# Swapped key columns in a shared tile, slabs split at other times, and a shorter hand-over from attention to merge

## The chip, the cores and the metric

The kernel runs on one core of one Trainium2 chip. The metric is the device time of one execution in microseconds (us). Kernels are compared by the median of several executions. A core has five engines that run side by side and meet at semaphores: TensorE (PE, matmuls), VectorE (DVE), ScalarE (ACT), GpSimd (POOL) and SyncE (SP, which here issues all transfers from HBM). All data is fp32. A matrix product is made of three matmuls: each operand is split into a high part, rounded for the matrix unit, and a low part, the rest; high x high, high x low and low x high are added in PSUM.

## The reference

Two networks run one after another on 512 tokens of width 1024, each with two layers. Cut to what matters here:

```python
def first_block(x, ...):                       # two layers
    u = rmsnorm(h, attn_norm[l])
    h = h + hybrid_mixer(u, ...)               # three attentions, gates, w_o
    u = rmsnorm(h, mlp_norm[l])
    h = h + square(relu(u @ w_up[l])) @ w_down[l]

# hybrid_mixer, its end
g = sigmoid(gates)
merged = (g[:, :, 0] * (o_a @ w_a) + g[:, :, 1] * (o_b @ w_b) + g[:, :, 2] * (o_c @ w_c))
return merged @ w_o

def hybrid_layer(x, w_in, ...):                # second network, two layers
    h = x @ w_in
    sb_cols, mla_cols, rwkv_cols = split(h)
    mix = concat([stick_breaking(sb_cols), mla_mixer(mla_cols), rwkv7_mixer(rwkv_cols)]) @ w_o
    x = layer_norm(ALPHA * x + mix)
    u_act, u_gate = split(x @ ffn_w_up)
    return layer_norm(ALPHA * x + (gelu(conv(u_act)) * u_gate) @ ffn_w_down)

# mla_mixer, its start: 192 + 128 + 32 columns
c_q, c_kv, k_rope = split(cols, [MLA_Q_LORA, MLA_Q_LORA + MLA_KV_LORA])
k_rope = apply_rope(k_rope, cos, sin)          # [t1*cos - t2*sin, t2*cos + t1*sin]
```

## The kernel before

The activations lie with the 1024 features on partitions, as eight chunks of 128 x 512 tokens. The program is a row of blocks, one after another; at the end of a block all engines meet. A first-network layer has a projection block, an attention block (the tiles of q, k and v come from the projection), a merge block (gates, the three branch products, w_o) and an MLP block. A second-network layer has a projection block, an attention block (stick-breaking and MLA), a recurrence block (RWKV) and a block with w_o, layer norm and the feed-forward part. Semaphores are of two sets that blocks use in turn; a block's end clears the set that was just used.

**Slabs.** Weights come from HBM in slabs of 128 x 2048 (1 MB), in a ring of two to four buffers named raw_a, raw_c, raw_f, raw_p or raw_d by the stage. For each slab ScalarE writes the high part (w_hi), and VectorE or GpSimd the low part (w_lo, raw minus w_hi); then PE uses it. The first two slabs of a block (AHEAD = 2) are fetched and split in the block before. For the second network's projection this is done by fetch_next2 (SyncE: parameters, then two slabs), next_hi2 (ScalarE, line 464) and next_lo2 (VectorE, line 469).

**Projection of the second network** (lines 1508 to 1745). Eleven slabs in the order SLABS2 hold two tiles of 128 output columns each; tile n of the list TILES is 24 matmuls (lines 396 to 398). Slab 1 holds the two tiles of MLA's query columns: cq tile 0 is 128 columns, tile 1 is 64 query columns, then the 32 key columns for rope on partitions 64 to 95, then 32 of zeros. Slab 2 holds the tile ckv and the tile krs, which is zeros but for the 32 key columns with halves swapped. Rope of the key is kr * cos + krs * sin, on VectorE (lines 1729 to 1731). ScalarE evicts each tile from PSUM (lines 1637 and 1641); GpSimd makes the low part of every slab from the third on (line 1685). LORA_AT, KK_AT, KKROOT_AT and CHAIN_AT say after which tile the side work of the recurrence is done.

**Attention of the first network** (lines 825 to 1085). 36 units of two heads and 128 queries go through a pipeline; a step of its loop has unit s0 at the logits, s1 at the exponentials, s2 at the scaling and turn of the weights, s3 at the values, s4 at the output. GpSimd multiplies the weights by the inverse denominators (line 1019, semaphore scaled), PE turns them (line 939, for dilated units 936), ScalarE or VectorE copies them to pt, PE multiplies by the values (line 960), ScalarE and VectorE keep high and low parts of the output (lines 1001 and 1072). The last two units are of the top-k attention, 512 keys wide. SyncE fetches the two first slabs of the merge block once the last dilated unit's logits are done.

**Start of the merge block.** PE first counts all banks up by one, so that waits can be written as if each bank had been used once. ScalarE writes the high part of the first 1024 columns of slab 0 (FIRST), then of the rest; VectorE the low parts (line 1219); PE waits for the first low part (part_lo).

**End of a second-network layer.** Eleven down slabs; slab m is split when PE has used slab m - 2 (split_down_hi, split_down_lo, with a row mean taken off by down_mean). Then, in layer 0, ScalarE splits the two next slabs behind the last down slab's split; VectorE adds the down product into h chunk by chunk (line 2950) and makes their low parts behind the first and the third addition. ScalarE squares h (line 2823), GpSimd adds up six of the squares (line 2836), PE sums over features (line 278), and the inverse root goes out through line 299 on. The end of the first network's last MLP block is built alike, with the low parts ahead of all additions.

## Time and profile before

| | us |
|---|---|
| median of three runs | 3522.18 |
| lowest, highest | 3518.57, 3523.44 |
| profiled execution, its time | 3520.51 |
| profiled execution, its span | 3518.7 |
| PE busy in it | 3375.3 (96%) |
| DVE, ACT, POOL busy | 1708.7, 1353.9, 982.5 |
| granted PE clock, mean | 0.976 |

All times in a view are microseconds from the start of the span. A matmul of 512 columns is listed with 0.39 us, but they overlap: at full clock one starts every 0.227 us, at half clock every 0.427. A row of the timeline has start, length, engine, line, instruction, out<-in, shapes, count, and in brackets how long the engine stood idle before it and what ended that. A "q" behind the engine means its sequencer, as for SyncE's transfers.

### The profile page before, as it was taken

The numbers are of one execution on the slowest core, as the hardware profiler recorded it, in microseconds if no ns is written. First come the engines' busy times: TensorE is split into PE (matmuls) and PEld (weight loads), VectorE is DVE, ScalarE is ACT, GpSimd is POOL, SyncE is SP. The second block draws the span as 40 slices with busy tenths as digits, with TensorE's granted clock in tenths as the row PEclk, the third lists the DMA queues.
The fourth block names the chain that finished last, engine by engine and source line by source line (L and its number), as shares of the span: only waits on it lengthen the run. The fifth ranks groups of instructions, "written<-read, shape, count | busy, mean of one in ns | idle before, by whom it ended". The sixth has DMA issues, their size and how long they took to land. (4 is left out here: it accounts for less than half of the span.)

```text
span 3518.7 us, 55538 instructions
## 1 busy us (share of the span) xinstructions
PE 3375.3 (96%) x22968; PEld 2773.4 (79%) x22968; DVE 1708.7 (49%) x2662; ACT 1353.9 (38%) x2059; POOL 982.5 (28%) x641
## 2 busy tenths in 40 slices
PE   8989999999999899999999999899998999899998
PEld 6777787888777778878887759888887768898887
DVE  4887334404249753441312656454454466454454
ACT  4646323313255453332224353343324443243322
POOL 2325002434433330034444341141102332232100
PEclk9999999999999999999999999899999999999999
DMA  3200222222222012223232200212222200012222
GB/s 141 91 30 27 89 102 86 96 96 96 96 96 72 1 54 100 102 85 107 92 110 105 72 1 4 76 58 95 96 96 91 84 13 3 29 73 105 95 96 72
DMA packets 38820, 267.04 MB, mean 76 GB/s; under 512 B 4800, under 2 KB 5184, under 8 KB 7616
## 3 DMA queue, kind: packets, MB, share of 16 engines
q1 hardware_dynamic: 38592, 263.74, 21.1%
q8 instruction: 174, 2.85, 0.3%
q14 instruction: 54, 0.44, 0.0%
HBM read 261.63 MB, written 2.10 MB: 75 GB/s over the span
## 5 line engine op out<-in xcount | busy, mean ns | idle before, releaser
L1418 POOL TENSOR_TENSOR w_lo_f<-raw_f,w_hi_f 128x2048 fp32r<-128x2048 f32 x60 | 275.9, 4598 | 384.6 <-ACT w_hi_f L384 384.6
L396 PE MATMUL ps<-u_hi,w_hi_d 128*128 128x512 f32 (+1 forms) x768 | 290.6, 378 | 7.8 <-POOL u_lo L2842 6.2
L398 PE MATMUL ps<-u_hi,w_lo_d 128*128 128x512 f32 (+1 forms) x768 | 286.8, 373 | 0.0
L397 PE MATMUL ps<-u_lo,w_hi_d 128*128 128x512 f32 (+1 forms) x768 | 286.7, 373 | 0.0
L384 ACT ACTIVATE w_hi_f<-raw_f 128x2048 fp32r<-128x2048 f32 x64 | 121.9, 1908 | 255.1 <-PE ps L398 243.8
L396 PE MATMUL ps<-u_hi,w_hi_f 128*128 128x512 f32 x512 | 201.7, 394 | 6.6 <-POOL u_lo L334 6.6
L607 POOL TENSOR_TENSOR w_lo_a<-raw_a,w_hi_a 128x2048 fp32r<-128x2048 f32 x30 | 137.9, 4600 | 229.3 <-ACT w_hi_a L603 229.3
L397 PE MATMUL ps<-u_lo,w_hi_f 128*128 128x512 f32 x512 | 201.1, 393 | 0.0
L398 PE MATMUL ps<-u_hi,w_lo_f 128*128 128x512 f32 x512 | 201.1, 393 | 0.0
L396 PE MATMUL ps<-hid_hi,w_hi_f 128*128 128x512 f32 x512 | 199.2, 389 | 0.0
L397 PE MATMUL ps<-hid_lo,w_hi_f 128*128 128x512 f32 x512 | 199.2, 389 | 0.0
L398 PE MATMUL ps<-hid_hi,w_lo_f 128*128 128x512 f32 x512 | 199.2, 389 | 0.0
L1445 DVE TENSOR_TENSOR hid<-hid 128x512 f32<-128x512 f32 x64 | 116.1, 1814 | 145.1 <-ACT hid L1394 144.0
L396 PE MATMUL ps<-u_hi,w_hi_a 128*128 128x512 f32 x432 | 172.7, 400 | 6.3 <-POOL u_lo L334 6.3
L396 PEld LDWEIGHTS ps<-u_hi,w_hi_d 128*128 128x128 f32 x768 | 146.1, 190 | 36.1 <-POOL u_lo L2842 8.1
L398 PE MATMUL ps<-u_hi,w_lo_a 128*128 128x512 f32 x432 | 169.5, 392 | 0.0
L397 PE MATMUL ps<-u_lo,w_hi_a 128*128 128x512 f32 x432 | 169.2, 392 | 0.0
L397 PEld LDWEIGHTS ps<-u_lo,w_hi_d 128*128 128x128 f32 x768 | 146.5, 191 | 25.6 <-issue 0.5
L398 PEld LDWEIGHTS ps<-u_hi,w_lo_d 128*128 128x128 f32 x768 | 146.3, 190 | 25.0
L2854 POOL TENSOR_TENSOR hid_lo<-ge,hid_hi 128x512 f32 (+1 forms) x44 | 57.2, 1300 | 385.2 <-ACT hid_hi L2799 385.2
L396 PE MATMUL ps<-u_hi,w_split_c 128*128 128x512 f32 x384 | 151.0, 393 | 7.3 <-DVE w_split_c L1219 7.3
L687 ACT ACTIVATE ps<-ps 32x512 f32<-32x512 f32 x208 | 117.3, 564 | 103.6 <-PE ps L398 53.6
(441 smaller groups left out, 8600.1 us busy)
## 6 DMA issues: line engine op xcount, KB each, us to landing
raw_d<-in_w SPq DMA_DIRECT2D x70, 1024.0 KB, 4.8
raw_f<-in_w SPq DMA_DIRECT2D x64, 1024.0 KB, 4.8
raw_c<-in_w SPq DMA_DIRECT2D x40, 1088.0 KB, 5.0
raw_a<-in_w SPq DMA_DIRECT2D x36, 1024.0 KB, 4.9
raw_p<-in_w SPq DMA_DIRECT2D x24, 1024.0 KB, 4.8
wo_raw<-in_w SPq DMA_DIRECT2D x4, 1024.0 KB, 6.1
cst<-in_cst SPq DMA_DIRECT2D x1, 2112.0 KB, 10.2
h<-in_x SPq DMA_DIRECT2D x8, 256.0 KB, 4.6
```

What stands on the lines that cost most here:

```text
L384: nc.scalar.activation(hi[:, k % 2, 0:width], raw[:, k % raw.shape[1], 0:width], ACT.Copy).then_inc(S["w_hi"], 1)
L396: nc.tensor.matmul(out, w_hi, x_hi, start=start, stop=False)
L397: nc.tensor.matmul(out, w_hi, x_lo, start=False, stop=False)
L398: return nc.tensor.matmul(out, w_lo, x_hi, start=False, stop=stop)
L607: eng.tensor_tensor(WA_lo[:, i % 4, :], WA_raw[:, i % 4, :], WA_hi[:, i % 3, :].bitcast(F32), ALU.subtract)\
L687: nc.scalar.activation(halves[32 * q:32 * q + 32, i % 2, :], src[32 * o:32 * o + 32, :], ACT.Copy).then_inc(S["swapped"], 1)
L1418: nc.gpsimd.tensor_tensor(WF[2][:, k % 2, :], WF[0][:, k % 2, :], WF[1][:, k % 2, :].bitcast(F32), ALU.subtract).then_inc(S["w_lo"], 1)
L1445: nc.vector.tensor_tensor(x, x, x, ALU.mult).then_inc(S["relu_kept"], 1)
L2854: nc.gpsimd.tensor_tensor(at(hid2_lo, k), ge, at(hid2_hi, k).bitcast(F32), ALU.subtract)\
```

## The change

There are five edits.

1. The 32 swapped key columns go into the zeros of cq tile 1 (partitions 96 to 127), and the tile krs is dropped from TILES. The host lays the weights out as before; slab 1 is now fetched in two transfers, all but the last 32 of each 256 columns, and those 32 from slab T2_KRS // 2. The sine table is fetched to partitions 96 to 127 as well. Slab 2 holds one tile; slab 3's low part is made by VectorE. The places of the recurrence's side work move up by one tile, but for LORA_AT, SUM_AT and ROOT_AT.
2. In the first attention VectorE scales the last two units (BY_DVE), not GpSimd.
3. ScalarE and VectorE split the first 1024 columns of merge slab 0 within the last steps of the attention block. PE no longer waits for part_lo.
4. SyncE, not PE, counts the banks at the start of the merge block, ahead of come_ahead.
5. At the end of second-network layer 0, the parameters for NORM_GAIN are copied ahead of the down slabs' loop; the first next slab is split behind down slab 9 (NEXT_AT), the second one on ScalarE behind the last down matmul's slab_used and on VectorE behind the last addition.

```diff
@@ fetch_next2, next_hi2
             for i in range(AHEAD):
-                sy.dma_start(WP_raw[:, i, :], d["w2"][layer:layer + 1, SLABS2[i], :, 0:2048].rearrange("a p c -> p (a c)"))\
-                  .then_inc(S["ahead"], 16)
+                to = WP_raw[:, i, :].rearrange("p (k c) -> p k c", c=256)
...
+                if SLABS2[i] == T2_CQ // 2:
+                    sy.dma_start(to[:, :, 0:SWAP_TO], cols(T2_CQ // 2, 0, SWAP_TO)).then_inc(S["ahead"], 16)
+                    sy.dma_start(to[:, :, SWAP_TO:256], cols(T2_KRS // 2, SWAP_AT, RD)).then_inc(S["ahead"], 16)
+                else:
+                    sy.dma_start(to, cols(SLABS2[i], 0, 256)).then_inc(S["ahead"], 16)
-            act.wait_ge(S["ahead"], 16 * (AHEAD + 1))
+            act.wait_ge(S["ahead"], 16 * (AHEAD + 2))
@@ first attention, PE / ACT / POOL / DVE
+                            if k in BY_DVE:
+                                pe.wait_ge(S["scaled_dve"], 2 * BY_DVE.index(k) + 1 + cs[-1] // n)
...
+                        if s2 == len(units) - 4:
+                            act.wait_ge(S["ahead"], 32)
+                            nc.scalar.activation(WC[1][:, 0, 0:FIRST], WC[0][:, 0, 0:FIRST], ACT.Copy).then_inc(S["first_hi"], 1)
...
+                        if k in BY_DVE:
+                            continue
...
+                            if k in BY_DVE:
+                                x, w = exps(k)
+                                dve.wait_ge(S["den_ready"], k + 1)
+                                for e in range(2):
+                                    nc.vector.tensor_scalar(x[:, e, 0:w], x[:, e, 0:w], per_unit(INV_AT, k)[:, e:e + 1], None, ALU.mult)\
+                                      .then_inc(S["scaled_dve"], 1)
+                            if k == len(units) - 1:
+                                dve.wait_ge(S["first_hi"], 1)
+                                nc.vector.tensor_tensor(WC[2][:, 0, 0:FIRST], WC[0][:, 0, 0:FIRST], WC[1][:, 0, 0:FIRST].bitcast(F32),
+                                                        ALU.subtract)
@@ merge block
+                    banks_counted(sy)
                     come_ahead(sy)
...
-                    for b in range(8):
-                        pe.sem_inc(full[b], 1)
-                        pe.sem_inc(read[b], 1)
...
-                                if (it, q, j) == (0, 0, 0):
-                                    pe.wait_ge(S["part_lo"], 1)
@@ projection of the second network
-            TILES = [2 * k + half for k in SLABS for half in range(2)]
+            TILES = [2 * k + half for k in SLABS for half in range(2) if 2 * k + half != T2_KRS]
...
-            LORA_AT, KK_AT = [4 + p for p in range(PAIRS)], [9 + p for p in range(PAIRS)]
+            LORA_AT, KK_AT = [4 + p for p in range(PAIRS)], [8 + p for p in range(PAIRS)]
...
-            CHAIN_AT = [13, 15, 17, 19]
+            CHAIN_AT = [12, 14, 16, 18]
...
+                        if n == AT[T2_CKV]:
+                            i = HALF + 1
+                            dve.wait_ge(S["w_hi"], i + 1)
+                            nc.vector.tensor_tensor(WP_lo[:, i % 3, :], WP_raw[:, i % 3, :], WP_hi[:, i % 2, :].bitcast(F32),
+                                                    ALU.subtract).then_inc(S["slab_lo_dve"], 1)
@@ end of a second-network layer
                         split_down_hi(act, m)
+                        if m == NEXT_AT and layer < DEPTH - 1:
+                            next_hi2(act, 0)
...
-                        for i in range(AHEAD):
-                            next_hi2(act, i)
+                        next_hi2(act, 1)
...
                         split_down_lo(dve, m)
-                    nc.vector.tensor_copy(small[:, NORM_GAIN:NORM_GAIN + 2 * DC], prm[:, P2_LN2G:P2_LN2G + 2 * DC])\
-                      .then_inc(S["kept_prm"], 1)
+                        if m == NEXT_AT and layer < DEPTH - 1:
+                            next_lo2(dve, 0)
...
-                        if n in (0, 2) and layer < DEPTH - 1:
-                            next_lo2(dve, n // 2)
+                    if layer < DEPTH - 1:
+                        next_lo2(dve, 1)
```

VectorE at the end of the first attention and the start of the merge block, before. sc_68 and sc_69 are the weights of units 34 and 35, L1048 the logits' eviction, L1072 low parts of outputs, w_split_c the parts of merge slab 0 and 1.

```order
L1048 ISA small 128x1
L1072 TENSOR_TENSOR o_lo<-ps,o_hi 128x128
L1084 RECIPROCAL small<-small 128x2
L1072 TENSOR_TENSOR o_lo<-ps,o_hi 128x128
L1084 RECIPROCAL small<-small 128x2
L1072 TENSOR_TENSOR o_lo<-ps,o_hi 128x128 x4
L887 UNCONDITIONAL_BRANCH
L1213 UNCONDITIONAL_BRANCH
L1219 TENSOR_TENSOR w_split_c<-raw_c,w_split_c 128x1024
L1219 TENSOR_TENSOR w_split_c<-raw_c,w_split_c 128x1152
```

The same place in the changed kernel.

```order
L1072 ISA small 128x1
L1096 TENSOR_TENSOR o_lo<-ps,o_hi 128x128
L1108 RECIPROCAL small<-small 128x2
L1113 TENSOR_SCALAR sc_68<-sc_68,small 128x512 x2
L1096 TENSOR_TENSOR o_lo<-ps,o_hi 128x128
L1108 RECIPROCAL small<-small 128x2
L1113 TENSOR_SCALAR sc_69<-sc_69,small 128x512 x2
L1117 TENSOR_TENSOR w_split_c<-raw_c,w_split_c 128x1024
L1096 TENSOR_TENSOR o_lo<-ps,o_hi 128x128 x4
L903 UNCONDITIONAL_BRANCH
L1240 UNCONDITIONAL_BRANCH
L1245 TENSOR_TENSOR w_split_c<-raw_c,w_split_c 128x1152
```

Four scalings came in, and the first half of the split went from behind the block's end to ahead of the last four low parts.

VectorE at the end of second-network layer 0, before: L2565 is the low part of a down slab, L469 of a next slab, L2950 an addition into h.

```order
L2565 SCALAR_TENSOR_TENSOR w_lo_d<-raw_d,small,w_hi_d 128x1024 x2
L2946 COPY small<-prm 128x16
L2950 SCALAR_TENSOR_TENSOR h<-h,ps 128x512
L469 TENSOR_TENSOR w_lo_p<-raw_p,w_hi_p 128x2048
L2950 SCALAR_TENSOR_TENSOR h<-h,ps 128x512 x2
L469 TENSOR_TENSOR w_lo_p<-raw_p,w_hi_p 128x2048
L2950 SCALAR_TENSOR_TENSOR h<-h,ps 128x512 x5
```

The same place in the changed kernel, with the mean of down slab 10 left in.

```order
L2604 SCALAR_TENSOR_TENSOR w_lo_d<-raw_d,small,w_hi_d 128x1024 x2
L482 TENSOR_TENSOR w_lo_p<-raw_p,w_hi_p 128x2048
L2591 TENSOR_REDUCE small<-raw_d 128x2
L2594 TENSOR_SCALAR small<-small 128x2
L2604 SCALAR_TENSOR_TENSOR w_lo_d<-raw_d,small,w_hi_d 128x1024 x2
L2992 SCALAR_TENSOR_TENSOR h<-h,ps 128x512 x8
L482 TENSOR_TENSOR w_lo_p<-raw_p,w_hi_p 128x2048
```

The first next slab's low part now stands ahead of the work on down slab 10, the second one behind all eight additions.

SyncE at the same layer's end, before and then changed.

```order
L2637 DMA raw_d<-in_w 128x2048
L455 DMA prm<-in_prm 128x165
L458 DMA raw_p<-in_w 128x2048 x2
L2633 UNCONDITIONAL_BRANCH
L1541 UNCONDITIONAL_BRANCH
```

```order
L2676 DMA raw_d<-in_w 128x2048
L462 DMA prm<-in_prm 128x165
L472 DMA raw_p<-in_w 128x2048
L469 DMA raw_p<-in_w 128x8x224
L470 DMA raw_p<-in_w 128x8x32
L2672 UNCONDITIONAL_BRANCH
```

The second slab became two transfers with eight pieces per partition each.

## Rows read from the trace of the kernel before

**Rows 1.** The page, busy time, share and instructions of each engine.
```profile
PE 3375.3 (96%) x22968; PEld 2773.4 (79%) x22968; DVE 1708.7 (49%) x2662; ACT 1353.9 (38%) x2059; POOL 982.5 (28%) x641
```
**Rows 2.** PE's waits: total us, times, longest.
```profile
PE ps L278 <- POOL qsum L2836: 6.5, 2, 5.9
```
**Rows 3.** Timeline, ACT, projection of second-network layer 0.
```profile
1914.09 0.60 ACT L1637 ACTIVATE cq<-ps 128x512 f32<-128x512 f32 x1 [2.38 <-PE ps L398]
...
1919.52 0.60 ACT L1637 ACTIVATE ckv<-ps 128x512 f32<-128x512 f32 x1 [2.52 <-PE ps L398]
```
**Rows 4.** Timeline, low parts on POOL and DVE, and DVE's idle stretch.
```profile
1865.56 4.49 DVE L469 TENSOR_TENSOR w_lo_p<-raw_p,w_hi_p 128x2048 fp32r<-128x2048 f32 x2 [71.90 <-ACT w_hi_p L464]
...
1916.57 4.58 POOL L1685 TENSOR_TENSOR w_lo_p<-raw_p,w_hi_p 128x2048 fp32r<-128x2048 f32 x1 [6.18 <-ACT w_hi_p L1622]
...
1933.80 0.75 DVE L1707 SCALAR_TENSOR_TENSOR rw_in<-ps,prm,rw_in 128x511 f32<-128x511 f32 x1 [28.99 <-ACT rw_in L1641]
```
**Rows 5.** Timeline, attention's end and merge's start, layer 0; last a group by form.
```profile
338.78 1.03 SPq L222 DMA_DIRECT2D raw_c<-in_w  x2
...
351.44 0.60 ACT L1005 ACTIVATE pt<-ps 128x512 f32<-128x512 f32 x1 [1.36 <-PE ps L939]
...
353.14 6.19 POOL L1019 TENSOR_SCALAR sc<-sc,small 128x512 f32<-128x512 f32 x4 [1.35 <-DVE small L1084]
353.38 0.66 PE L960 MATMUL ps<-pt,cv 128*64 128x128 f32 x8
...
359.97 1.97 PE L960 MATMUL ps<-pt,av 128*64 128x128 f32 x32
...
362.36 0.29 DVE L1072 TENSOR_TENSOR o_lo<-ps,o_hi 128x128 fp32r<-128x128 f32 x1 [0.58 <-ACT o_hi L1001]
...
365.57 0.76 PE L396 MATMUL ps<-u_hi,w_split_c 128*128 128x512 f32 x1 [3.63 <-DVE w_split_c L1219]
...
L1740 DVE TENSOR_SCALAR asig<-asig,prm 128x512 f32<-128x512 f32 x8 | 3.9, 487 | 0.3
```
**Rows 6.** Stretches: us, busy PE, PEld, DVE, ACT, POOL, then clock, DMA, GB/s.
```profile
362.00:365.50 3.50, 0.00 (x0) 0.00 (x0) 1.75 (x3) 2.81 (x4) 0.00 (x0) 0.95 0.00 0
365.50:368.60 3.10, 3.03 (x7) 2.48 (x8) 2.63 (x2) 2.75 (x2) 0.00 (x0) 0.50 0.30 51
```
**Rows 7.** Timeline and a transfer's time, end of second-network layer 0.
```profile
2649.79 0.34 SPq L2637 DMA_DIRECT2D raw_d<-in_w  x1
...
2669.04 2.48 DVE L2565 SCALAR_TENSOR_TENSOR w_lo_d<-raw_d,small,w_hi_d 128x1024 fp32r<-128x1024 f32 x2 [6.00 <-ACT w_hi_d L2546]
...
2688.08 0.39 PE L398 MATMUL ps<-hid_hi,w_lo_d 128*128 128x512 f32 x1
...
2699.68 0.16 DVE L299 TENSOR_SCALAR small<-ps 128x4 f32<-128x4 f32 x1 [7.28 <-PE ps L278]
...
raw_d<-in_w SPq DMA_DIRECT2D x70, 1024.0 KB, 4.8
```
**Rows 8.** Timeline, end of second-network layer 1, PE and DVE.
```profile
3502.75 0.39 PE L398 MATMUL ps<-hid_hi,w_lo_d 128*128 128x512 f32 x1
...
3507.38 0.16 DVE L299 TENSOR_SCALAR small<-ps 128x4 f32<-128x4 f32 x1 [3.51 <-PE ps L278]
```
**Rows 9.** Transfers in 917.9:918.5 (132 B), 1850.2:1852.2 (660 B), 1860:1862.5 (8 KB); an issue near 2671.6.
```profile
q1 hardware_dynamic: 144, 0.02, 27.2%
...
q1 hardware_dynamic: 161, 0.12, 18.0%
...
q1 hardware_dynamic: 145, 1.06, 100.8%
...
prm<-in_prm SPq DMA_DIRECT2D x1, 82.5 KB, 1.9
```
**Rows 10.** Timeline, end of the first network, ACT and PE.
```profile
1863.61 3.72 ACT L464 ACTIVATE w_hi_p<-raw_p 128x2048 fp32r<-128x2048 f32 x2 [5.32 <-DMA raw_p<-in_w]
...
1879.51 1.02 PE L278 MATMUL ps<-cst,hid 128*128 128x2 f32 x8 [1.57 <-POOL hid L289]
```

73 lines of the change are left out of this document (45 added, 28 removed).

## The prediction, made before the changed kernel was run

> **What bounds the kernel now.** I read the page first: TensorE (PE) is busy for 96% of the span [rows 1]. So time can be won in two ways only: fewer matmuls, or fewer microseconds in which PE stands still. The list of PE's waits (who waited, for whom, in total, times, longest) tells which stops are large and what releases them; the sum at the end of a layer of the second network stands there with 6.5 us in two stops, 5.9 of it in one [rows 2]. Two stops of one line that differ so much are a question by themselves. Then I read the timeline at the four places that the diff names, engine by engine, and lastly the granted clock. The profiled execution took 3520.5 us (span 3518.7, 1.8 around it). The sum below is made against 3520.5, which is 1.7 under the median of the three runs shown.
>
> **Part 1, one tile fewer in each second-network projection.** The tile of swapped key columns was 24 matmuls of 128x512. Evictions of neighbouring plain tiles start 5.43 us apart, 1914.09 to 1919.52 [rows 3]; that is 24 matmuls at full clock, one every 0.227 us. PE has no stop inside this stage, so each layer loses 5.4 us: 2 x 5.4 = **10.9 us**. ScalarE's eviction of the tile goes too, under PE and worth nothing. The risk is the supply of weights: slab 2 now holds one tile, so slab 3 is wanted 5.4 us sooner. Its low part was made by GpSimd from 1916.57 to 1921.15 [rows 4]. PE would want it when the key tile is done and the first two decay matmuls are through, after 1919.5: up to 1.6 us late. The change gives this subtraction to VectorE, which is idle for 29.0 us before 1933.80 and does two such slabs in 4.49 us, 2.3 each [rows 4]: 1916.6 to 1918.9, in time, with 0.6 us or more to spare. All later slabs keep their distance to PE. Rope of the key part moves one tile earlier on the same idle VectorE. No cost.
>
> **Part 2, the tail of the first attention.** The last two units are scaled by GpSimd in one run of 6.19 us, four instructions of 1.55 [rows 5]. PE turns each half as it comes, and its last values end at 361.94, 359.97 + 1.97. VectorE does a 128x512 multiplication by a column in 0.49 us [rows 5]. Its scaling of unit 34 can start at 353.1, where GpSimd's did, and end at 354.1; unit 35 follows two microseconds later and stays ahead of PE. Then PE is the pace: it is free at 354.04 (353.38 + 0.66), turns 0.65 + 0.65 for unit 34, values 0.66, turns 0.65 + 0.65 for unit 35, and does the last values in 1.97, which ends at 359.3. **2.6 us** less in each layer. New on VectorE behind it is the first half of the merge split, about 1.2 us; behind that stand only the low parts of outputs whose matmuls end later still. New on ScalarE is the high part, 1.06 us, ahead of a copy at 351.44 for which ScalarE had waited 1.36 us [rows 5]: it fits. Its data must have landed; the transfer is issued at 338.78 [rows 5], eleven microseconds before.
>
> **Part 3, the start of the merge block.** Now: PE's last matmul ends at 361.94, the last low part at 362.65 (362.36 + 0.29), then ScalarE copies, VectorE subtracts, and PE starts at 365.57 [rows 5]. With both done before the block, PE waits for the block's start alone and for the first count of a bank. ScalarE's first copy began 0.30 us after the last low part, behind SyncE's counts, so I put PE at +0.4. 365.57 - 362.65 - 0.4 = **2.5 us** per layer. The sixteen counts cost PE nothing before, since it waited for the split anyway; left on PE they would now show. On SyncE they stand ahead of come_ahead, for which ScalarE's first copy waits. No row gives a count's price; between nothing and 0.1 us each I allow the 0.1, 1.6 us in all. Then the second half's copy and subtraction (1.2 and 1.4 us) end near +4.5 us, and PE wants them after 24 matmuls, at +5.8. Hidden, by 1.3 us, and with it what stands behind on SyncE, the first refill of a slab. If the cover is gone, PE stops for the difference, once a layer. Parts 2 and 3: 2 x 5.1 = **10.2 us**.
>
> **Part 4, the clock behind it.** In 362 to 365.5 PE did nothing, and in 365.5 to 368.6 the granted clock was 0.50 (1.2 GHz), 7 matmuls in 3.1 us [rows 6]. At full clock these seven take 1.6. With the change PE stands still for only about 1.1 us there. I take it that the fall goes away: 2 x 1.4 = **2.8 us**. If not, this term is nothing. The Trainium skill ("TensorE: Matmul & The Clock Gate", Part 1) says that the throttled state is the default and that activity releases it; by that rule, the trace agrees, the fall follows the idle stretch, and the sum is the one with 2.8.
>
> **Part 5, from layer 0 to layer 1 of the second network.** In layer 0 the last matmul starts at 2688.08 and the token sum is read at 2699.68, 11.60 us later [rows 7]. In layer 1, where nothing is split ahead, it is 3502.75 to 3507.38, 4.63 us [rows 8]. The difference, **7.0 us**, is what the two slabs cost at this place: their two subtractions stand between VectorE's additions of h, and ScalarE's squares stand behind the copies. After the change the first slab is split under matmuls one slab earlier, ScalarE does the second before the first square is due, and VectorE's second subtraction stands behind the last addition: 2.3 us inside the 4.6 in which PE sums. So layer 0 should look like layer 1. The transfers are issued some 21 us sooner, right behind that of down slab 10. What is late next is down slab 10: ScalarE and VectorE touch it only after the early split. Its low part ends at 2671.52 now [rows 7]; PE wants it 48 matmuls, 10.9 us, before its last one ends, at 2677.4. Working back through a low part, a high part and a mean of up to 2.5 us each [rows 7] and the early split (1.9 [rows 10] and 2.3 [rows 4]), the transfers must have landed by 2665.7. Slab 10's transfer is issued at 2649.79 and takes 4.8 [rows 7], to 2654.6. Of the 11.1 us left, the parameter block wants about 0.3, a whole slab 2.5 and a second one 2.5: 6 us of room for pieces to be slower.
>
> **Part 6, a slab in 2048 pieces.** The second slab ahead is now 1024 pieces of 896 bytes and 1024 of 128 bytes instead of 128 rows of 8 KB. No transfer of such pieces is in the trace. The nearest packets [rows 9]: of 8 KB, 100.8% of 16 engines for 2.5 us and about 129 packets, 0.31 us each; of 660 bytes, 18.0% of 16 x 2.0 us for 128 and a few others, about 0.04; of 132 bytes, 27.2% of 16 x 0.6 us over 144, about 0.02. An engine gets 64 of either kind. Low end: 64 x (0.048 + 0.018) = 4.2 us against 8 x 0.31 = 2.5, so 1.7 more; in the best case nothing is lost or gained, since the bytes are the same. High end: the 128-piece parameter block took 1.9 us from issue to landing [rows 9]; if pieces came at that pace whatever the engines do, 2048 take 30 us, 28 more. I take 2.5, near the packets' own times, since those are measured at work and most of the 1.9 us of a small transfer is there for a large one too. Between the layers this hides (6 us of room). At the end of the first network it doesn't: ScalarE waited 5.32 us for this very transfer and started at 1863.61, VectorE's two subtractions and additions follow, and PE waits at 1879.51 for GpSimd's sum of what they give [rows 10]. So **2.5 us are lost** there, once. The Trainium skill ("DMA: Bandwidth & Descriptors", Specifications) speaks against this edit: it wants 512 bytes and more for line rate. The trace's 132-byte packets move far fewer bytes per time than the 8 KB ones, which agrees; taken to its end it makes the 128-byte pieces the slow ones, which is rival (a). The constants' transfer, now in three parts, is issued ahead of the slabs' and wanted behind the last down slab's split: hidden, unless its parts cost more than the slab's.
>
> **The sum.** 10.9 + 10.2 + 2.8 + 7.0 - 2.5 = 28.4; 3520.5 - 28.4 = **3492.1 us**.
>
> **Rivals.** (a) Pieces are moderately slow, 6 to 12 us more than the slab was. The end of the first network loses that, and above 6 us the room between the layers is gone too. At 6: 3.5 less gain, 3496; at 10: 7.5 and 4 of a stall at slab 10, 3504. For it: four times as many packets in flight per engine as anywhere in the trace; against it: their short times. (b) Slower than before: the pieces come one after another at the parameter block's pace. 28 lost at the end of the first network, and 28 - 6 = 22 of stall at down slab 10; 30.9 gained otherwise, so 3520.5 - 30.9 + 50 = 3540. It decides from about 18 us more per transfer. (c) The tail of the attention doesn't shorten, because VectorE's scaling waits for something I don't see or another bank comes late: parts 2 to 4 shrink by 5.2 and the clock's 2.8, 3500. (d) The clock falls at the merge as before, 3494.9; inside the forecast's range.
>
> **How the numbers follow.** My forecast, with (d) in it: 0.80. (a): 0.09. (c): 0.07. (b): 0.02. The edits give nothing that can be seen, since the clock's falls shift or an unseen wait takes their place: 0.02. The clock rises at a different moment after each of the eight or so stops, and half a microsecond to 1.5 either way at each is 3 us in all; with the runs' own 2 us, and (d), the forecast reaches from 3486 to 3497. To leave no more than 2 in 10 out, the range goes on to (c): **3486 to 3501**. A measurement tells 0.2%, 7 us, from no change: faster 0.95 (forecast, (a), (c)), same 0.03, slower 0.02.
>
> **What would show it.** 352 matmuls of line 396 on w_hi_p become 336 and the stage has no stop of PE. The run of GpSimd at 353 is gone and PE's stop before the first merge matmul is near 1.1 us with the clock at 1.0 behind it. The stop of 5.9 us at the layer's end is about 0.6. ScalarE's wait at the end of the first network shows the pieces' price directly; if it grows by more than 6 us, part 6 was wrong. A new stop of PE at the last down slab would mean the same between the layers.

## The result, and the profile after

| | before | changed |
|---|---|---|
| median of the runs, us | 3520.38 (4 runs) | 3484.69 (4 runs) |
| lowest, highest | 3515.36, 3523.44 | 3483.63, 3485.89 |
| ratio, 95% interval | | 0.990 (0.9888 to 0.9912) |
| profiled execution, its span | 3518.7 | 3482.6 |
| PE busy in it | 3375.3 | 3354.8 |
| granted PE clock, mean | 0.976 | 0.979 |

The changed kernel is 35.7 us faster. The forecast was 3492.1, from 3486 to 3501: the direction was right, the gain was put at 28.4, and the time lies 1.3 us under the range. The spans of the two profiled executions differ by 36.1.

Every place that the forecast named changed about as it said. First the waits of PE (total us, times, longest), which answer to [rows 2], and the matmuls of the projection by form:

```profile
PE ps L402 <- SPq L229: 2.1, 2, 1.0
...
PE ps L284 <- POOL hid L295: 3.1, 2, 2.5
...
PE ps L284 <- POOL qsum L2876: 1.1, 2, 0.5
```
```profile
L402 PE MATMUL ps<-u_hi,w_hi_p 128*128 128x512 f32 x336 | 137.0, 408 | 8.0 <-POOL u_lo L1534 8.0
```

The stops of 5.9 us and of 3.6 us are gone; the one ahead of the sum at the end of the first network grew by 0.9 (1.57 in [rows 10], 2.50 now), and the 336 matmuls are one tile per layer fewer. Timeline of the changed kernel, end of the attention and start of the merge in layer 0 (columns as in [rows 5], to which it answers):

```profile
355.75 0.88 DVE L1113 TENSOR_SCALAR sc<-sc,small 128x512 f32<-128x512 f32 x2
...
356.55 1.22 DVE L1117 TENSOR_TENSOR w_split_c<-raw_c,w_split_c 128x1024 fp32r<-128x1024 f32 x1
...
357.60 1.97 PE L979 MATMUL ps<-pt,av 128*64 128x128 f32 x32
...
359.99 0.29 DVE L1096 TENSOR_TENSOR o_lo<-ps,o_hi 128x128 fp32r<-128x128 f32 x1 [0.58 <-ACT o_hi L1020]
...
360.61 0.50 PE L402 MATMUL ps<-u_hi,w_split_c 128*128 128x512 f32 x1 [1.04 <-SPq L229]
```

PE's last values end at 359.57; the merge starts 0.33 us after the last low part (359.99 + 0.29), where 2.92 lay before. The clock behind it stays at its upper level, which answers to [rows 6]:

```profile
360.50:363.90 3.40, 3.29 (x14) 2.74 (x15) 1.17 (x1) 2.38 (x2) 0.00 (x0) 1.00 0.00 0
```

End of second-network layer 0, as [rows 7]: from the last down matmul to the reading of the sum 4.66 us, 11.60 before.

```profile
2664.34 0.39 PE L404 MATMUL ps<-hid_hi,w_lo_d 128*128 128x512 f32 x1
...
2665.26 1.02 PE L284 MATMUL ps<-cst,qsum 128*128 128x2 f32 x8 [0.53 <-POOL qsum L2876]
...
2669.00 0.16 DVE L305 TENSOR_SCALAR small<-ps 128x4 f32<-128x4 f32 x1 [1.11 <-PE ps L284]
```

End of the first network, as [rows 10]. SyncE's three issues, ScalarE's wait for them, and PE's stop, now 2.50 us:

```profile
1840.14 0.35 SPq L472 DMA_DIRECT2D raw_p<-in_w  x1
...
1840.53 0.44 SPq L469 DMA_DIRECT2D raw_p<-in_w  x1
...
1841.01 0.58 SPq L470 DMA_DIRECT2D raw_p<-in_w  x1
...
1848.49 3.72 ACT L477 ACTIVATE w_hi_p<-raw_p 128x2048 fp32r<-128x2048 f32 x2 [6.27 <-DMA raw_p<-in_w]
```
```profile
1864.37 1.43 PE L284 MATMUL ps<-cst,hid 128*128 128x2 f32 x8 [2.50 <-POOL hid L295]
```

To get the terms I compared the start of every PE matmul with that of the same matmul before, and read where the difference (the offset) changes. It changes by these amounts at the places of the edits:

| term, us | forecast | read from the two traces |
|---|---|---|
| two tiles fewer | 10.9 | 10.9 |
| tail of the attention, two layers | 5.2 | 6.3 |
| start of the merge, two layers | 5.0 | 5.3 |
| clock behind it | 2.8 | 2.8 |
| end of layer 0, second network | 7.0 | 7.0 |
| slab in pieces, end of the first network | -2.5 | -1.5 |
| sum | 28.4 | 30.8 |

Two of these rows hold clock as well. At the end of layer 0, before:

```profile
2694.39 1.84 PE L278 MATMUL ps<-cst,qsum 128*128 128x2 f32 x8 [5.92 <-POOL qsum L2836]
```

Behind this stop the 24 matmuls of the sum took 5.29 us until the sum was read, at half clock (it is low from 2693.1), and 3.74 after (2665.26 to 2669.00): 5.4 of the 7.0 are the shorter stop, 1.6 are clock. Of the -1.5 at the end of the first network 0.9 is the stop, and 0.6 is that the clock falls nearer to the start of the sum. At full clock the rows therefore add up to 27.0 (10.9 + 6.3 + 5.3 + 5.4 - 0.9).

**5.3 of the 36.1 us stand in none of these rows.** They come at stops that are alike in both kernels. In what follows, a fall is the moment at which the granted clock goes to its lower level (1.2 GHz, 0.50), and a low stretch is the time until it is back at 1.00. The plainest is the stop ahead of the first network's MLP block in layer 0. Stretches before (590.5 on) and after (584.8 on); the columns are as in [rows 6]:

```profile
590.50:593.80 3.30, 1.92 (x16) 1.86 (x16) 1.12 (x4) 0.84 (x2) 0.28 (x1) 1.00 0.00 0
593.90:597.20 3.30, 1.12 (x4) 0.72 (x4) 1.71 (x4) 0.85 (x2) 0.17 (x1) 0.50 0.14 20
597.30:600.60 3.30, 2.15 (x5) 1.80 (x6) 3.22 (x5) 1.97 (x4) 2.65 (x2) 0.50 0.88 355
600.70:604.10 3.40, 3.40 (x9) 2.63 (x8) 2.86 (x5) 1.86 (x4) 2.43 (x2) 0.50 0.55 234
```
```profile
584.80:588.20 3.40, 2.23 (x19) 2.02 (x18) 0.77 (x3) 0.79 (x2) 0.00 (x0) 1.00 0.00 0
588.30:591.60 3.30, 0.01 (x1) 0.00 (x0) 2.83 (x4) 1.89 (x3) 1.34 (x2) 0.50 0.42 97
591.70:595.00 3.30, 3.30 (x8) 2.62 (x9) 3.26 (x6) 1.49 (x3) 2.39 (x2) 0.50 1.00 420
595.10:598.40 3.30, 3.30 (x16) 2.67 (x15) 2.34 (x4) 1.57 (x3) 1.57 (x2) 1.00 0.21 89
```

PE waits 3.33 us for the same subtraction in both. Before, the clock is at its lower level from 593.9 to 604.1, 10.2 us; after, from 588.2 to 595.1, 6.8 us. The work resumes at 598.45 and 591.64, so 5.7 us of it ran at half clock before and 3.4 after. That alone is 1.1 us, with no edit near it. Over all stops the clock is low for 172.3 us before and 148.6 after (the last stretch counted to its end, 2 us behind the last instruction).

### The profile page after: what moved, and what is told of

It is laid out like the page before. It is cut to its first block and busy times, and to the rows that moved or that the text cites. A ratio compares the mean times of both kernels' runs of the same rounds, so it can differ in the third digit from the quotient of the medians.

```text
span 3482.6 us, 55438 instructions
## 1 busy us (share of the span) xinstructions
PE 3354.8 (96%) x22920; PEld 2758.1 (79%) x22920; DVE 1715.5 (49%) x2672; ACT 1351.9 (39%) x2057; POOL 958.1 (28%) x631
## 5 line engine op out<-in xcount | busy, mean ns | idle before, releaser
L700 ACT ACTIVATE ps<-ps 32x512 f32<-32x512 f32 x208 | 117.3, 564 | 103.7 <-PE ps L404 53.7
L396 DVE TENSOR_TENSOR w_lo_d<-raw_d,w_hi_d 128x2048 fp32r<-128x2048 f32 x44 | 106.3, 2416 | 104.0 <-ACT w_hi_d L390 103.4
```

What stands on the lines that cost most here:

```text
L396: nc.vector.tensor_tensor(lo[:, k % 2, 0:width], raw[:, k % raw.shape[1], 0:width], hi[:, k % 2, 0:width].bitcast(F32), ALU.subtract).then ...
L700: nc.scalar.activation(halves[32 * q:32 * q + 32, i % 2, :], src[32 * o:32 * o + 32, :], ACT.Copy).then_inc(S["swapped"], 1)
```

## The experiments

All are built from the changed kernel where nothing else is said. Its time over two sets of four runs is 3484.69 and 3485.14; differences below are against 3484.9. The kernel before was run beside each set, with medians of 3520.1, 3517.2 (the four kernels on the end of layer 0, the tail, the split and the counts), 3518.1 (the two shifts and the first two candidates) and 3522.2 us (the rest). So differences across sets are sure to 2 or 3 us only, and for the second set may be that much too small; where less matters, the reading goes by the traces.

### Each kernel once more

The question is whether the 5.3 us come and go between executions, or belong to the programs.

> The kernel before, once more, for a second trace of it. The trace shown of before has 22 half-clock stretches, 172 us in all; the changed kernel has 20, 149 us. Two of the seven 3.4 us pieces fewer lie at the merge, where the change removes the stop, one at the end of layer 0 and one at the program's end; three net lie behind stops that the change doesn't touch (593.9 to 604.1 in before, 588.2 to 595.1 after, for one). Theory L (these are luck: how far the clock falls behind one and the same stop differs between executions of one program): this trace has some unchanged stops with a stretch longer or shorter by 3.4 us than the first trace, and PE's starts drift against it by 1 to 1.7 us at each; the single times spread over 4 us or more. Theory D (the falls belong to the program): the same 22 stretches with the same lengths, 172 us, and times within 2 us of 3520.5.

> The changed kernel once more, in more rounds. Theory L: the half-clock stretches behind unchanged stops differ by 3.4 us here and there from the first trace of it, and the median lies between 3483 and 3490, with single times up to 5 us apart. The gain that the terms carry is then 30.8 (tile 10.9, tail 6.3, start of merge 5.3, clock there 2.8, layer's end 7.0, less 1.5 for pieces) and the rest, up to 5 us, comes and goes. Theory D: the same stretches, 149 us, and a median of 3484.7 within 1.5; the 5.3 us that my terms don't hold are then a steady part of the gain.

Before again: 3521.08 (10 runs, 3513.69 to 3523.03). Changed again: 3485.14 (4 runs, 3484.07 to 3488.76), ratio 0.9899 (0.9883 to 0.9916). Of the 22 low stretches of before 19 have the same length in the second trace, of the 20 of the changed kernel 18. The stop shown above has 10.2 us in both traces of before and 6.8 in both of after:

```profile
596.20:606.30 10.10, 6.78 (x18) 5.15 (x18) 7.96 (x12) 5.04 (x8) 5.49 (x4) 0.50 0.55 208
```
```profile
589.30:596.00 6.70, 3.40 (x8) 2.75 (x9) 6.23 (x9) 3.41 (x6) 3.86 (x3) 0.50 0.72 262
```

Two others of the changed kernel are longer by 3.4 us in its second trace (17.1 where it was 13.7 at 1865 us, 6.8 where it was 3.4 at 2070), and its span is 3487.0. Neither theory holds as it was put: most falls belong to the program, two or three per execution move. The gain of 35 us is steady all the same, by the medians.

### Moving one stop and nothing else

Five or ten matmuls without a use go into the merge block of layer 0, some 140 us ahead of the stop shown above. Nothing else differs, so the stop only comes later.

```diff
                                 b = bank_to_fill(pe, jobs, ("gate", q, j), it)
+                                if (layer, it, q, j) == (0, 2, 0, 0):
+                                    for _ in range(5):        # and 10
+                                        nc.tensor.matmul(ps[:, b, :], w_hi[:, 0, :], u_hi[:, 0, :], start=True, stop=True)
```

> The changed kernel with 5 extra matmuls of 512 columns, without a use, in merge layer 0 (about 1.13 us at full clock), long before the stop at its end. Nothing else differs, and every later stop has the same cause and length. In ten traces the half-clock stretch behind this stop is 6.83 us long where the work resumes 2.8 to 3.7 us after the clock's fall, and 10.24 where it resumes 4.3 to 6.6 after it. In the changed kernel it resumes 3.39 after it. Phase theory: now 4.5 after it, so 10.24, and PE is 1.13 + 1.15 = 2.3 us later behind this stretch; behind the next one (950 us, 3.46 now) 2.3 to 2.9 later; at the end anything from 0 to 5, not the plain 1.1. Rival (the falls are the program's, a shift is only a shift): all stretches as before and 1.1 us more at every place.

> The same with 10 extra matmuls, 2.27 us. Phase theory: the work resumes 5.7 after the fall, stretch 10.24, or the clock falls one step later and the work resumes 2.2 after it, stretch 6.83: by both PE is 2.8 us later behind it, only 0.5 more than with 5; and at later stops the stretches differ from those of the changed kernel at several places, in both directions. Rival: 2.3 us more at every place, twice the shift of 5.

With 5: 3489.04 (3487.27 to 3490.81), with 10: 3491.36 (3487.31 to 3493.53). So 1.13 us of matmuls cost 4.1, and 2.27 cost 6.4, by medians of different sets, each sure to 2 or 3 us; what the clock does is read from the traces. The stop is the same 3.33 us, and the clock low for 10.2 us (587.1 to 597.4, and with 10 matmuls 587.9 to 598.1):

```profile
587.20:593.90 6.70, 2.75 (x8) 2.11 (x9) 5.04 (x8) 2.44 (x4) 2.92 (x2) 0.50 0.46 155
594.00:597.30 3.30, 3.30 (x9) 2.56 (x9) 3.25 (x5) 1.90 (x3) 1.81 (x2) 0.50 0.73 308
597.50:600.70 3.20, 3.20 (x16) 2.65 (x15) 0.69 (x1) 0.58 (x1) 0.55 (x1) 1.00 0.02 5
```
```profile
592.26 0.77 PE L402 MATMUL ps<-u_hi,w_hi_f 128*128 128x512 f32 x1 [3.33 <-POOL u_lo L340]
```

This work resumes 5.1 us after the fall, where it was 3.4. Against the changed kernel, PE was 0.97 us early ahead of the five matmuls in this execution, 0.16 late behind them, 1.37 late behind this stop and 2.43 late behind the next one. So 1.13 became 2.34 at the first stop, where the phase theory said 2.3, and 3.40 at the second, where it said 2.3 to 2.9; from there on the falls differ in both directions. With ten it is 2.26, then 3.23 behind both stops. The rival, 1.1 us at every place, is out. In the fourteen traces without extra matmuls under the stops, the five block changes of this kind (near 590, 950, 1510, 1870 and 2670 us) all follow one order, by how long after the fall the block's first product starts:

| start after the fall, us | clock low for, us |
|---|---|
| 2.5 to 3.9 | 6.8 |
| 4.0 to 7.0 | 10.2 |
| 8.2 to 10.7 | 13.7 |
| 10.8 to 13.6 | 17.1 |
| 16.0 | 20.5 |

So what a stop costs in clock goes by its moment as well as by its length, and 1 us more or less ahead of it changes that. The Trainium skill ("TensorE: Matmul & The Clock Gate", Part 1) has the low state as the default that activity releases; the traces agree, and they add that the release comes later for the same stop when its moment shifts.

### The first edit alone

The tile krs, the whole-slab transfer, GpSimd's split of slab 3 and the old places of the side work are put back.

```diff
-            TILES = [2 * k + half for k in SLABS for half in range(2) if 2 * k + half != T2_KRS]
+            TILES = [2 * k + half for k in SLABS for half in range(2)]
```

> The changed kernel with the first edit undone alone: the tile of swapped key columns is back, slab 1 comes in one transfer, GpSimd splits slab 3, the side work is one tile later. Terms theory: 10.9 slower for the two tiles, 1.5 faster at the end of the first network for the whole slab: 3484.7 + 9.4 = 3494.1. If the edit brings more than its matmuls (a better place of the side work, fewer clock falls behind it), 3497 or more; if the early supply of slab 3 costs something hidden in the trace, under 3492.

3494.03 (3490.76 to 3496.53), 9.1 slower; 9.4 was expected. Within the 2 or 3 us of such a difference this edit holds no hidden work.

### What the pieces cost

Slab 1 in one transfer (this leaves out the swapped columns, so its result is not that of the reference; only its time is read), and, as the other end, slab 0 in eight transfers of 128-byte pieces.

```diff
-                if SLABS2[i] == T2_CQ // 2:
-                    sy.dma_start(to[:, :, 0:SWAP_TO], cols(T2_CQ // 2, 0, SWAP_TO)).then_inc(S["ahead"], 16)
-                    sy.dma_start(to[:, :, SWAP_TO:256], cols(T2_KRS // 2, SWAP_AT, RD)).then_inc(S["ahead"], 16)
-                else:
-                    sy.dma_start(to, cols(SLABS2[i], 0, 256)).then_inc(S["ahead"], 16)
+                sy.dma_start(to, cols(SLABS2[i], 0, 256)).then_inc(S["ahead"], 16)
```

> The changed kernel with slab 1 of the second network's projection fetched in one transfer of 8 KB rows; its swapped columns are then the zeros of the host's layout, so that rope of the key lacks its second half. Terms theory: the transfer lands about 1.0 us earlier and one issue of 0.5 us less stands ahead, PE's stop at the end of the first network goes from 2.5 back to about 1.6 us, and 3483.2 (1.5 less) is read; nothing changes between the layers, where the transfers land 11 us ahead of their need. Forecast's own price for the pieces: 2.5 less, 3482.2. If the pieces slow other transfers as well (the third slab behind them), more than 3 us less.

> The changed kernel with slab 0 ahead of the second network's projection fetched in eight transfers of 1024 pieces of 128 bytes each, instead of one of 128 rows of 8 KB; slab 1 as in the changed kernel. One look. By the row of 132-byte packets (0.02 us each, 64 more per engine and transfer) it lands 8 x 1.2 = 9.4 us after the engines begin, 7 later than a whole slab; the eight issues of 0.6 us take 4.7 of it. By the change's own slab (1024 + 1024 pieces landed 1.0 us later than a whole one, half of it the second issue) 8 x 0.5 = 4 to 5 us later. If small pieces come one after another at the pace of a parameter block (1.9 us for 128), more than 100.

Whole slab: 3483.57 (3482.96 to 3485.82), 1.3 less. SyncE issues both at 1839.57 and ScalarE starts 7.16 us later, against 8.35 (1840.14 to 1848.49) in the changed kernel: the pieces cost 1.2 us, 0.6 of it the added issue. PE's stop is 1.35.

```profile
1839.57 0.82 SPq L468 DMA_DIRECT2D raw_p<-in_w  x2
...
1846.73 3.72 ACT L473 ACTIVATE w_hi_p<-raw_p 128x2048 fp32r<-128x2048 f32 x2 [5.09 <-DMA raw_p<-in_w]
```

Only pieces: eight issues in 5.99 us, 0.75 each where an issue of a whole slab takes 0.35, and ScalarE starts 13.34 us after the first issue, 5.0 later than in the changed kernel. One execution took 3491.78, 6.9 more; there is only this one.

```profile
1840.92 5.99 SPq L473 DMA_DIRECT2D raw_p<-in_w  x8
1846.95 0.75 SPq L469 DMA_DIRECT2D raw_p<-in_w  x1
1847.74 0.90 SPq L470 DMA_DIRECT2D raw_p<-in_w  x1
1854.26 3.72 ACT L478 ACTIVATE w_hi_p<-raw_p 128x2048 fp32r<-128x2048 f32 x2 [11.27 <-DMA raw_p<-in_w]
```

So 1 MB in 8192 pieces of 128 bytes costs 5.0 us more than in 128 rows, and the issuing alone takes 5.6 more, 6.0 against 0.35. Whether an issue of many pieces takes long by itself or waits for those ahead of it isn't shown: the two issues of slab 1 behind them also take longer here, 0.75 and 0.90 where they took 0.44 and 0.58.

### The end of layer 0 alone

```diff
-                        if m == NEXT_AT and layer < DEPTH - 1:
-                            next_hi2(act, 0)
...
-                        next_hi2(act, 1)
+                        for i in range(AHEAD):
+                            next_hi2(act, i)
...
+                        if n in (0, 2) and layer < DEPTH - 1:
+                            next_lo2(dve, n // 2)
```

> The changed kernel with the order at the end of second-network layer 0 put back: both next slabs split by ScalarE behind the last down slab's use, their low parts between VectorE's additions. The parameters' copy stays early, and so do the transfers. Terms theory: from the last down matmul to the reading of the token sum 11.6 us in place of 4.66, so 7.0 slower, 3484.9 + 7.0 = 3491.9. If half-clock stretches behind it, or behind later stops that are the same in both, grow too, up to 3 more; if they shrink, as little as 4 more than 3484.9.

3489.76 (3487.92 to 3491.19), 4.9 slower by the medians, not 7.0. The way from the last down matmul to the sum is 2668.21 to 2678.02, 9.81 us, so the place itself costs 5.2 and not 7.0 (3.6 as a longer stop, 1.6 as half clock in the sum behind it):

```profile
2672.73 0.56 PE L284 MATMUL ps<-cst,qsum 128*128 128x2 f32 x2 [4.14 <-POOL qsum L2875]
```

The transfers still come early here, and ScalarE begins 10.5 us ahead of the last down matmul (2657.75), where it began 8.7 ahead in the kernel before (2679.37, behind a wait for the transfers); the forecast's 7.0 is right for the whole edit, and about 1.8 of it is the earlier fetch.

### Tail, first half of the split, and bank counts, each undone

```diff
-            BY_DVE = (len(units) - 2, len(units) - 1)
+            BY_DVE = ()
```

> The changed kernel with the last two units of the first attention scaled by GpSimd again. Terms theory, by the two traces of before and after: PE's last values end 3.1 and 3.3 us later in the two layers, 3491.3. Forecast's own size: 2.6 each, 3490.1. The first half of merge slab 0 is then split under the wait for GpSimd, so the start of the merge doesn't change. A rival, that clock falls behind unchanged stops carry part of what the trace shows as the tail's gain: under 3488, or above 3494.

3495.81 (3494.45 to 3495.88), 10.9 slower where 6.3 was expected. PE waits for GpSimd as before, in four stops (the last two are shown), but here the clock falls amid them and the last values run at half of it, 3.68 us in place of 1.97:

```profile
360.70 1.09 PE L958 MATMUL ps<-cst,sc 128*128 128x128 f32 x4 [0.30 <-POOL sc L1043]
362.24 1.12 PE L958 MATMUL ps<-cst,sc 128*128 128x128 f32 x4 [0.45 <-POOL sc L1043]
363.28 3.68 PE L979 MATMUL ps<-pt,av 128*64 128x128 f32 x32
```

In the kernel before the fall came 3 us after these values. The rival of the expectation (above 3494) holds: an edit's worth depends on where the clock's falls lie in the kernel that it is made in.

```diff
 # the first half split in the merge block (ScalarE, VectorE), and on PE:
+                                if (it, q, j) == (0, 0, 0):
+                                    pe.wait_ge(S["part_lo"], 1)
```

> The changed kernel with both halves of merge slab 0 split within the merge block, and PE waiting for the first low part; SyncE still counts the banks. Terms theory: PE starts 2.65 us later in each layer and the clock falls there again for 1.4 us of cost, so 8.1 slower, 3493.0. ScalarE's first copy now waits for SyncE's sixteen counts as well (0.06 us each by the changed trace), up to 1 us per layer more: 3495. If the clock at the merge doesn't fall, 3490.

```diff
-                    banks_counted(sy)
                     come_ahead(sy)
...
+                    for b in range(8):
+                        pe.sem_inc(full[b], 1)
+                        pe.sem_inc(read[b], 1)
```

> The changed kernel with the sixteen bank counts back on PE. Theory: they are now the last thing ahead of PE's first merge matmul; at 0.06 us each, as SyncE's are spaced in the changed trace, PE starts 0.7 us later in each layer, 3484.9 + 1.4 = 3486.3, and no clock fall. If a count costs PE more (0.1 us), 3487.5. If the longer stop makes the clock fall behind it, up to 3489. Rival: nothing that can be seen, since the counts run while PE's last matmuls drain.

First half in the merge block: 3492.85 (3490.39 to 3496.22), 8.0 slower, as expected. Counts on PE: **3497.51** (3496.26 to 3498.64), 12.6 slower where 1.4 was expected. Here PE's first merge matmul comes 2.82 us after the last low part, though the low part that it needs has been there since 358.3; the profile names no releaser, only issue:

```profile
360.53 0.29 DVE L1096 TENSOR_TENSOR o_lo<-ps,o_hi 128x128 fp32r<-128x128 f32 x1 [0.58 <-ACT o_hi L1020]
361.12 1.16 ACT L1196 ACTIVATE w_split_c<-raw_c 128x1152 fp32r<-128x1152 f32 x1 [0.69 <-SPq L235]
...
363.64 0.76 PE L402 MATMUL ps<-u_hi,w_split_c 128*128 128x512 f32 x1 [3.54 <-issue]
```

With the split alone put back, SyncE's counts delay ScalarE's copy by 0.94 (1.24 after the last low part, 0.30 before), and PE starts at 363.21:

```profile
359.31 0.29 DVE L1093 TENSOR_TENSOR o_lo<-ps,o_hi 128x128 fp32r<-128x128 f32 x1 [0.58 <-ACT o_hi L1020]
360.84 1.06 ACT L1189 ACTIVATE w_split_c<-raw_c 128x1024 fp32r<-128x1024 f32 x1 [1.63 <-SPq L235]
...
363.21 0.80 PE L402 MATMUL ps<-u_hi,w_split_c 128*128 128x512 f32 x1 [4.33 <-DVE w_split_c L1242]
```

The four kernels side by side, from the end of the last low part to PE's first merge matmul, layer 0:

| us | split in the merge block | split ahead |
|---|---|---|
| PE counts | 2.92 (before) | 2.82 |
| SyncE counts | 3.61 | 0.33 (changed) |

Two causes of the same length lay side by side: either edit alone gives 0.1 us there or costs 0.7, both give 2.6 per layer. The semaphore events of the traces show the counts themselves. With the counts on PE the sixteen go from 361.19 to 363.60, 2.4 us or 0.15 each, and PE's first matmul follows at 363.64; SyncE's go from 360.54 to 361.45 in the changed kernel, 0.06 each. In the kernel before, the first low part was ready at 365.28 and PE's sixteenth count was done at 365.37, so the counts, not the split, ended last, by 0.1 us; the view names the split because it leaves counts out. Of the 12.6 us the later starts are 5.0. The other 7.6 are in the main clock: it falls at the merge again (3.4 us, twice), the stretches at 592 and 951 us are 10.2 again, as in the kernel before, and half of PE's busy time in all low stretches is 58.5 us, against 49.6 and 52.9 in the two traces of the changed kernel.

### Is all of the 5.3 the clock's?

Both kernels get the same matmuls without a use under their stops (they are shown with the candidates below), to have fewer falls in both.

> The changed kernel with all the extra matmuls of the last one, and nothing else (its first network ends as in the changed kernel): 3 us or so above it. It is one half of a pair with the kernel before made alike: with fewer half-clock stretches in both, the difference of the two shows what the five edits are worth without the clock's share at unchanged stops. Sum of the terms as read in the traces: 30.7 (28.0 without the fall at the merge, 2.8).

> The kernel before with the same extra matmuls (and SyncE counting the banks of the MLP block). If the 5.3 us that my terms leave open are half-clock time behind unchanged stops, this pair differs by 27 to 32. If they are work of the edits that I have not seen, it still differs by 35 to 36.

Changed: 3469.42 (3467.42 to 3471.5). Before: 3507.33 (3502.28 to 3511.74). They differ by 37.9, outside both expectations (27 to 32, 35 to 36). The pair is not clean: in the kernel before, the clock is low for 142.3 us, in the changed one for 104.3, and before's fall now lies in the attention's tail, as in the experiment above. So I took the clock out by estimate instead: half of the time that PE is busy in the low stretches, summed over each whole trace.

| kernel | span | clock low | PE busy in it | half of that | span less that |
|---|---|---|---|---|---|
| before | 3518.7 | 172.3 | 117.3 | 58.6 | 3460.1 |
| before, again | 3521.2 | 176.0 | 123.3 | 61.7 | 3459.5 |
| changed | 3482.6 | 148.6 | 99.1 | 49.6 | 3433.0 |
| changed, again | 3487.0 | 155.4 | 105.7 | 52.9 | 3434.1 |
| before, filled | 3509.8 | 142.3 | 111.4 | 55.7 | 3454.1 |
| changed, filled | 3466.8 | 104.3 | 77.0 | 38.5 | 3428.3 |

Less the clock, the edits save 26.2 us in the plain kernels (3459.8 to 3433.6) and 25.8 in the filled ones. The terms read at full clock from the first pair of traces were 27.0, where this table has 27.1 (3460.1 to 3433.0). The forecast's terms without its clock term are 25.6; that this is so near is in part luck, since 1.6 of its 7.0 for layer 0 was clock, while its tail was too small and its pieces too dear. The clock gives 8.9 in the plain pair and 17.2 in the filled pair. This is an estimate (a latency that PE only waits out isn't halved); that both pairs agree within 0.4 us while their clock shares differ by 8 is what it rests on. Applied to the single experiments it is less exact: with the end of layer 0 undone it gives 3439.0, 5.4 above the changed kernel where the stop grew by 3.6, and with ten matmuls added 3437.4, 3.8 above where they take 2.3. So it is good to about 2 us; hidden work of 5 us is not left.

### Candidates

The first one treats the end of the first network as the change treats layer 0 of the second; the next ones put matmuls without a use where PE stands still anyway.

```diff
-                            for i in range(AHEAD):
+                            for i in range(AHEAD if layer < DEPTH - 1 else 1):
                                 (next_lo if layer < DEPTH - 1 else next_lo2)(dve, i)
...
+                    if layer == DEPTH - 1:
+                        next_lo2(dve, 1)
                     token_inverse(dve, jobs, "sum", Signal(dve_own))
```

> A candidate: at the end of the first network the second low part of the next slabs is taken behind VectorE's additions, as the change does at the end of second-network layer 0. VectorE's first addition comes 2.2 us earlier; the later ones are paced by PE. Theory: PE's stop of 2.5 us before the token sum becomes about 1.3, 1.2 us less; with the clock behind it the median is 3481 to 3486. Rival: GpSimd's chain of five additions of squares is the bound and nothing changes.

3481.06 (3479.2 to 3484.07), 3.8 less. PE's stop goes from 2.50 to 0.63 us.

```diff
+        def warm(b, w, n):
+            for _ in range(n):
+                nc.tensor.matmul(ps[:, b, :], w[:, 0:P], w[:, 0:512], start=True, stop=True)
...
+                        if hf == 0:
+                            warm(jobs.at["up", 0][0], WF[1][:, 0, :], 6)
```

> A candidate, the last one plus matmuls without a use at the head of the blocks whose first product waits for the normed input (projection and MLP blocks, 6 or 7 of 512 columns each), under the stop of 3.1 to 4.0 us that is there anyway; SyncE counts the MLP block's banks, so that PE is free for them. Theory: the clock comes back one step of 3.4 us earlier at four or five of the five such places that have a fall (588, 947, 1506, 1865, 2667 us), 1.7 us each: 7 to 8.5 less, 3475 to 3478. Rival A: matmuls at half clock under the stop don't bring it back, and the median stays within 1 of the last candidate's. Rival B: at half clock they last longer than the stop, PE starts later, and it is slower by 1 to 3.

3474.42 (3473.07 to 3475.38), 6.6 under the last one, with 38 extra matmuls. SyncE counts the banks of the MLP block here, so that PE is free for them; what that brings by itself was not tried. At 1863 us the clock is low for 6.8 us in place of 13.7, at 2663 for 3.4.

> The last candidate (extra matmuls at the heads of the blocks) with more of them: 13 under the stop of 4.3 us for the last pair of value slabs in each first-network projection, 12 under the 3.4 us ahead of the first turn of each attention, 3 under each stop of 1.2 us for the inverse roots but the first. Theory (a stop that is filled with matmuls lets the clock not fall or rise sooner): the falls at 219, 254, 1137 and 1172 us go, 1.5 to 3 each, 6 to 10 less than 3474.4 together, and up to 1.7 at each of the five block changes: 3460 to 3467. Rival: the fills delay the work behind them where the clock is down already, 3472 or more.

**3466.92** (3462.58 to 3467.3), ratio to before 0.9844 (0.9828 to 0.9861): 18 us under the changed kernel, and the fastest one here. The extra matmuls, and the product behind them:

```profile
586.98 2.93 PE L411 MATMUL ps<-w_hi_f 128*128 128x512 f32 x6 [0.76 <-POOLq L1453]
589.70 0.63 PE L404 MATMUL ps<-u_hi,w_hi_f 128*128 128x512 f32 x1
```

The clock doesn't fall any more near 219 and 254 us, but it does at 270.5, for 6.8 us, where it stayed up before; in layer 1 the falls of the attention (1138, 1172) go without such a one. Rows near 219 and 254 us:

```profile
219.00:223.00 4.00, 3.67 (x15) 3.68 (x16) 3.90 (x8) 1.08 (x2) 0.27 (x1) 1.00 0.00 0
250.00:254.00 4.00, 4.00 (x31) 3.65 (x31) 3.01 (x11) 1.72 (x9) 1.67 (x4) 1.00 0.00 0
```

It is low for 111 us in all, and the kernel has 106 matmuls more than the changed one. What of the 14.1 us each place brings wasn't tried one by one.

## Why the prediction missed, step by step

- **Part 1** held: 10.9, no stop of PE in the stage, slab 3 in time. Undone, it gave 9.1 of 9.4.
- **Part 2** was 1.1 too small. The forecast put the end of the last values at 359.3, and they ended at 359.57, which looks close; but the profiled execution of the changed kernel was 0.8 us behind that of before when it came to the attention (its first turn at 253.92, not 253.12). Set against the same matmuls, the tail is 3.1 and 3.2 us shorter, not 2.6. The forecast added up listed lengths (0.65 for four turns, 0.66 for eight values), but a listed length overlaps the next group: by their starts eight turns take 1.03 and eight values 0.58. From the start of the last eight values before unit 34's turns to the end of all it had 5.9 us, and the changed kernel takes 5.19 (354.38 to 359.57).
- **Part 3** had the right sum, 5.0 for 5.3, by a wrong price. "Between nothing and 0.1 us each I allow the 0.1": a count takes SyncE 0.06 and PE 0.15. "The sixteen counts cost PE nothing before, since it waited for the split anyway" does not hold: they ended 0.1 us after the split's first part, so PE would have been just as late without the split. The forecast came out right because both edits are made together.
- **Part 4** held where it looked, 2.8. The step that failed is the one behind it, in "how the numbers follow": clock shifts at unchanged stops were taken as noise, "3 us in all", either way. They are mostly fixed in a program; here they were worth 5.3 on one side (by the estimate above the clock is worth 8.9 in all: these 5.3, the merge's 2.8, 1.6 in layer 0's sum, less 0.6 at the end of the first network). With the 2.4 us by which the other terms were too small, that is more than the range allowed. The forecast also spoke of "eight or so stops", where the trace of before has 22 low stretches.
- **Part 5** held to 0.1 us. But what it called the cost of two slabs in VectorE's and ScalarE's way is 5.4 us of stop and 1.6 of half clock in the sum; and 5.2 of the 7.0 are the order, 1.8 the earlier fetch, which the forecast had put on the order alone.
- **Part 6** was 1.0 too dear. The packets' own times gave 1.7 more for the pieces; they took 1.2 with the added issue in it. The 2.5 was 0.8 put on top for what no row showed. The room between the layers was not needed: the low part of slab 10 ended at 2649.05, 4.6 us before PE wanted it.
- **The rivals**: (a) and (b) need pieces 6 or 18 us slower; (c) a tail that stays; (d) a fall at the merge. None came. A rival that was missing is the one that happened: the same stops at another phase. Its size could have been bounded from before's trace, where single stretches differ by 3.4 us, or 1 to 1.7 us of PE's work, at some ten stops.

## What to carry to other kernels

Sum the terms at full clock, and put the clock beside them as a term of its own with a wide range: every change of a microsecond ahead of a stop can lengthen or shorten the half-clock stretch behind it, at this stop and at all later ones. Where a stop is released by one thing, ask what else would have been just as late, since an edit of one of two equal causes shows nothing. A stop that can't be removed can be filled with matmuls that nobody reads; the fills here were cut to end about when the wait does, and no run tried a longer one.

## What the runs showed of the hardware that I had not expected

- Semaphore counts are not free on PE: sixteen take 2.4 us, on SyncE 0.9.
- A transfer in 128-byte pieces is slow to issue (0.75 us for 1024 pieces, 0.35 for a slab in 128 rows): 1 MB of only such pieces lands 5.0 us later, and its issues take 5.6 us more.
- Five matmuls of 1.13 us in all made the kernel 4.1 us slower (sure to 2 or 3 us by the medians; 3.40 behind two stops by the trace); 38 of the same form under stops made it 6.6 us faster, and 106 of them 14.1.
- At one and the same stop of 3.33 us the clock is low for 6.8 or for 10.2 us, depending on its moment.
